# Delta-rule projection: the first half chunk ahead of the small products, a weight split inside the convolution, and a store that is awaited one block later

## What is computed

```python
h = rms_norm(x, mix_norm_w[l])
proj = jnp.einsum('bsd,de->bse', h, w_in[l])
sb_qkv, gdn_qkv, gdn_z, gdn_b, gdn_a, gate_sb, gate_gdn = jnp.split(proj, offsets, axis=-1)
...
qkv = jax.nn.silu(causal_depthwise_conv(gdn_qkv, gdn_conv_w[l]))
...
gq = l2_normalize(gq)
gk = l2_normalize(gk)
beta = jax.nn.sigmoid(gdn_b.astype(f32)).transpose(0, 2, 1)
g = -(jnp.exp(gdn_a_log[l].astype(f32))
      * jax.nn.softplus(gdn_a.astype(f32) + gdn_dt_bias[l].astype(f32))).transpose(0, 2, 1)
o_gdn = gated_delta_rule_chunked(gq, gk, gv, g, beta).transpose(0, 2, 1, 3)
z = gdn_z.reshape(B, S, GDN_HEADS, GDN_HEAD_DIM).astype(f32)
o_gdn = (rms_norm(o_gdn, gdn_out_norm_w[l]) * jax.nn.silu(z)).reshape(B, S, GDN_WIDTH).astype(x.dtype)
```

## Time and profile before

| | us |
|---|---|
| runs: median (lowest to highest), 3 runs | 3376.21 (3370.66 to 3384.74) |
| the profiled execution | 3366.91 |
| its span, first to last instruction | 3365.1 |
| block of `delta_inputs` in the trace | about 1127.5 to 1344.6 |
| block of `delta_rule` in the trace | about 1344.6 to 1568 |

### The profile page before, as it was taken

How to read it: one execution, slowest core, us unless ns; L and a number is a source line. 1 busy time by engine, 2 the same in 40 slices (tenths; PEclk the granted TensorE clock), 3 DMA queues, 4 the chain that set the end, 5 groups by cost and what they waited for, 6 DMA issues and landing times. The chain is left out here.

```text
span 3365.1 us, 30753 instructions
## 1 busy us (share of the span) xinstructions
PE 2814.4 (84%) x10832; PEld 1866.2 (55%) x10832; DVE 1822.0 (54%) x3272; ACT 884.6 (26%) x1621; POOL 1216.2 (36%) x1236
## 2 busy tenths in 40 slices
PE   6999999999899898899999876675767676777777
PEld 5887577765677677898778732232323232322223
DVE  5762643344534564556243786765765566754443
ACT  2113232614446564324223211110111011111111
POOL 0000210000202241540001366666666666666665
PEclk7999999999999999999999988787889788878778
DMA  6452223200221133002223599999999999999998
GB/s 235 174 176 82 71 73 102 88 13 1 88 88 63 40 101 114 6 1 91 95 104 132 210 353 369 373 367 392 363 364 378 373 377 374 364 367 380 369 371 317
DMA packets 228770, 706.46 MB, mean 210 GB/s; under 512 B 23188, under 2 KB 25492, under 8 KB 227735
## 3 DMA queue, kind: packets, MB, share of 16 engines
q0 software_dynamic: 147456, 536.94, 41.6%
q1 hardware_dynamic: 81176, 167.76, 14.5%
HBM read 694.13 MB, written 10.49 MB: 209 GB/s over the span
## 5 line engine op out<-in xcount | busy, mean ns | idle before, releaser
L2825 PE MATMUL work_banks<-rows_over_split,sig 128*128 128x512 f32 x1024 | 520.1, 655 | 238.7 <-issue 170.3
L2825 PEld LDWEIGHTS work_banks<-rows_over_split,sig 128*128 128x128 f32 x1024 | 210.3, 208 | 538.1 <-issue 464.1
L219 DVE TENSOR_TENSOR weights_low<-weights_raw,weights_high 128x2048 fp32r<-128x2048 f32 x108 | 251.3, 2328 | 439.0 <-ACT weights_high L214 429.5
L2825 PE MATMUL work_banks<-weights_raw,sig 128*128 128x512 f32 x512 | 260.1, 666 | 175.7 <-issue 88.2
L2917 DVE CUSTOM_DVE_ANT_0 proj_banks<-rows_over_parts,work_banks 128x1024 f32<-128x1024 f32 x256 | 310.3, 1241 | 161.0 <-DMA rows_over_parts<-in_peer_u_dram,eidx 138.6
L277 PE MATMUL proj_banks<-h_low,weights_high 128*128 128x512 f32 x896 | 358.4, 400 | 30.5 <-DVE weights_low L219 12.9
L214 ACT CAST weights_high<-weights_raw 128x2048 fp32r<-128x2048 f32 x108 | 206.0, 1907 | 612.4 <-PE proj_banks L277 588.1
L277 PE MATMUL proj_banks<-h_high,weights_low 128*128 128x512 f32 x896 | 353.2, 394 | 0.0
L277 PE MATMUL proj_banks<-h_high,weights_high 128*128 128x512 f32 x896 | 352.9, 394 | 0.0
L2711 POOL DMA_INDIRECT rows_over_split<-in_peer_v_dram,eidx x256 | 241.0, 941 | 151.2 <-issue 71.5
L2825 PEld LDWEIGHTS work_banks<-weights_raw,sig 128*128 128x128 f32 x512 | 108.2, 216 | 323.9 <-issue 268.6
(11 more groups left out here) (490 smaller groups left out, 4902.9 us busy)
## 6 DMA issues: line engine op xcount, KB each, us to landing
weights_raw<-in_w_in_dram SPq DMA_DIRECT2D x36, 1024.0 KB, 5.1
weights_raw<-in_ret_w_in_dram SPq DMA_DIRECT2D x24, 1024.0 KB, 5.2
ret_gate<-in_mod_w_dram SPq DMA_DIRECT2D x20, 1024.0 KB
weights_raw<-in_fox_w_in_dram SPq DMA_DIRECT2D x16, 1024.0 KB, 5.3
weights_raw<-in_ret_w_out_dram SPq DMA_DIRECT2D x8, 1024.0 KB, 5.0
weights_raw<-in_peer_w_q_dram SPq DMA_DIRECT2D x8, 1024.0 KB, 5.3
ret_v<-in_mod_w_dram SPq DMA_DIRECT2D x4, 1024.0 KB
weights_raw<-in_fox_w_out_dram SPq DMA_DIRECT2D x4, 1024.0 KB, 5.1
```

The source lines that it names most:

```text
L219: nc.vector.tensor_tensor(wlo[h][:, :, :], raw[h][:, :, :], whi[h][:, :, :].bitcast(F32), ALU.subtract).then_inc(w_split[h], 1)
L2825: last = nc.tensor.matmul(pa[:, half, :], diag[:, s, e, :], v_row(s, e)[:, half * CW:(half + 1) * CW], start=(first and e == 0), stop=(las ...
```

## The change

Three places are rewritten.

1. In `delta_inputs` PE does half 0 of chunk 0 ahead of the small products. ACT and DVE do `split_second` of chunk 0 first of all.
2. On DVE `split_second` of chunk c + 1 stands between tiles 0 and 1 and tiles 2 and 3 of the convolution of chunk c. ACT's order in the loop stays.
3. SP no longer waits for `z_put` in `delta_inputs`. The semaphore is handed to `delta_rule`, where SP waits for it behind the load of the masks, and DVE ahead of its first write of `att`.

```diff
@@ delta_inputs, SP
                     sp.dma_start(z_away, zg[:, :, :]).then_inc(z_put, 16)
-                    sp.wait_ge(z_put, 16)
                     sp.wait_ge(o_put, 16)
@@ delta_inputs, PE (head_squares is only moved up)
+                    project_half(pe, 0, 0, parts)
                     pe.wait_ge(cw_loaded, 16)
...
                     for c in range(n):
-                        project_half(pe, c, 0, parts, c < QKV)
+                        if c:
+                            project_half(pe, c, 0, parts, c < QKV)
@@ delta_inputs, DVE
                     link = Steps(dve, vstep)
+                    split_second(low, 0)
                     dve.wait_ge(wba_high, 1)
...
-                    def convolve(c):
-                        for t in range(4):
+                    def convolve(c, tiles):
+                        for t in tiles:
...
                     for c in range(n):
-                        split_second(low, c)
                         split_next(low, c)
...
                         if c < QKV:
-                            convolve(c)
+                            convolve(c, range(0, 2))
+                        if c + 1 < n:
+                            split_second(low, c + 1)
+                        if c < QKV:
+                            convolve(c, range(2, 4))
@@ delta_inputs, ACT
                     link = Steps(act, astep)
+                    split_second(high, 0)
                     act.wait_ge(wba_loaded, 16)
...
                     for c in range(n):
-                        split_second(high, c)
+                        if c:
+                            split_second(high, c)
@@ delta_inputs and delta_rule
             stage_end(n)
+        return z_put
...
                     sp.dma_start(masks[:, :, :], a["inv_masks"]).then_inc(masks_loaded, 16)
+                    sp.wait_ge(z_put, 16)
...
                         dve.wait_ge(products_full, h + 1)
+                        if h == 0:
+                            dve.wait_ge(z_put, 16)
                         nc.vector.tensor_tensor(att[:, h, :, :], chunks(pb[:, 2, :]), dec[:, h % 2, :, :], ALU.mult)
```

More of the change, by code:

```diff
@@ L1975, in _, with head_squares @@
                 def _(pe):
+                    def head_squares(group):
+                        for i in range(4 * group, 4 * group + 4):
+                            pe.wait_ge(sq_ready, i + 1)
+                            if i >= 4:
+                                pe.wait_ge(ln_done, i - 3)
+                            nc.tensor.matmul(pa[:, i % 4, :], ones, sq[:, i % 4, :], start=True, stop=True
+                                             ).then_inc(ss_full, 1)
+                    project_half(pe, 0, 0, parts)
                     pe.wait_ge(cw_loaded, 16)
@@ L1988, in _ @@
                     last.then_inc(ba_full, 1)
-                    def head_squares(group):
-                        for i in range(4 * group, 4 * group + 4):
-                            pe.wait_ge(sq_ready, i + 1)
-                            if i >= 4:
-                                pe.wait_ge(ln_done, i - 3)
-                            nc.tensor.matmul(pa[:, i % 4, :], ones, sq[:, i % 4, :], start=True, stop=True
-                                             ).then_inc(ss_full, 1)
                     for c in range(n):
-                        project_half(pe, c, 0, parts, c < QKV)
+                        if c:
+                            project_half(pe, c, 0, parts, c < QKV)
                         if 2 <= c < 6:
@@ L2145, in delta_inputs, with delta_rule @@
             stage_end(n)
-    def delta_rule(qkv, sc, sig, osb):
+        return z_put
+    def delta_rule(qkv, sc, sig, osb, z_put):
         H, LV, HG = GDN_HEADS, 7, 4
@@ L3103, in build @@
                 sc = sbuf(st2, "gdn_cols", [P, GDN_HEADS, 5, TT])
-                delta_inputs(parts, qkv, sc, sig, osb, o_away, z_away, columns(a["w_in_2"][0], 7 * D + 2 * GDN_HEADS))
-                delta_rule(qkv, sc, sig, osb)
+                z_put = delta_inputs(parts, qkv, sc, sig, osb, o_away, z_away, columns(a["w_in_2"][0], 7 * D + 2 * GDN_HEADS))
+                delta_rule(qkv, sc, sig, osb, z_put)
                 ogt = x[:, :, :].rearrange("p t (b n) -> p (t b) n", b=2)
```

## The result

| | before | changed |
|---|---|---|
| five runs each: median (lowest to highest), us | 3376.21 (3370.66 to 3384.74) | 3353.85 (3347.24 to 3357.03) |
| profiled execution, us | 3366.91 | 3347.24 |
| block of delta_inputs, first DMA to first DMA of delta_rule | 217.15 | 197.24 |
| block of delta_rule, to the first DMA of gates | 218.89 | 218.78 |

The changed kernel takes 0.9931 of the time of the kernel before (95% interval 0.9919 to 0.9943; the two medians alone give 0.9934): 22.4 us less by the medians, and 19.2 to 27.3 us less by the interval. 3357.0 was forecast, 19.2 us less. The block of delta_rule before ends at 1563.5 in the trace; the "about 1568" given for it ahead of the prediction is too late.

What follows compares the result with a forecast made beforehand. PE was taken to bound delta_inputs, with gains only where it idles or runs at half clock. 6.2 + 5.5 + 1.6 + 5.9 = 19.2 us, so 3376.2 - 19.2 = 3357.0; range 3346 to 3367.

Steps and rivals of the forecast that it cites:

- The start: Start of delta_inputs: half 0 of chunk 0 runs early, the 24 small passes then at full clock; 6.2 us saved.
- Rival (c): Start of delta_inputs: half 0 starts early but not at full clock, 2.7 us less; 16.5 saved, 3359.7; chance 0.10.
- The split: Convolution in delta_inputs: PE no longer loses time to half 1's split; 5.5 us saved in chunk 1, 1.6 in chunk 6.
- The store: End of delta_inputs: the next block no longer waits for the last store; 5.9 us saved.
- Behind the store: Start of delta_rule: store and masks land in time for the first write of att at 1348.15; 0 lost.
- The cause of the late landing: Start of delta_rule: masks and store share SP's rings, consumed in ring order, so the masks land at 1346.4.
- Rival (a): delta_rule: PE's clock falls later, over heads behind the first, costing at most 3.2 us; 16.0 saved, 3360.2; chance 0.15.
- Rival (b): delta_rule: masks come early and the clock stays up, 2.6 to 3.6 us more; 22.3 saved, 3353.9; chance 0.10.
- Rival (d): Chunks 1 to 5 of delta_inputs: the convolution becomes the bound, PE waits for banks; slower, 3382; chance 0.02.

Runs made afterwards that it cites:

- the store alone: Only SP's wait for the store moved into delta_rule, against the kernel before: ratio 0.9987 (0.9977 to 0.9997).
- the start alone: Only the start of delta_inputs changed, split and store wait left as they were, against the kernel before: ratio 0.9976 (0.9966 to 0.9986).

## Why the prediction was right, point by point

**The start.** 6.2 us were summed, 6.6 measured with this part alone. The passes ran at full clock as forecast (0.69 us for three). The wait of 0.77 us for DVE's copy stayed. Rival (c) did not come: an idle time of 1.20 us left the clock at 1.00, as the 1.54 us elsewhere had.

**The split.** 5.5 and 1.6 us were summed, 5.7 and 1.85 measured. The terms came from the distance between two rows, which holds both the idle time and the matmuls at half clock behind it; 3.85 and 1.51, the idle times alone, would have been 2.2 us short of the measured sum.

**The store.** 5.9 us were summed and 5.93 measured (6.70 less 0.77). The next block's first instruction stands 0.77 us behind the issue, as forecast (0.8).

**Behind the store.** The masks were to land 8.45 us behind the store's issue; by their issue at 0.77 and 7.5 us to landing it was 8.3. This term was right in size, and its landing just covered. What it was covered by was not: I let PE start delta_rule at half clock as before, with a first write of `att` 9.4 us behind the start. PE started at full clock and would have released the write at 6.6, as it did where the masks were awaited late, so the masks became the late one. The write came at 8.9, 0.5 us better than forecast, with POOL as the releaser. The forecast had named this row's releaser as a sign that it was wrong, but with a later time, not an earlier one. That delta_rule took what it took before, 218.8 against 218.9 us, is luck and not the reckoned cover: 0.5 us won at the first write, 1.2 lost by the clock over head 1, and 0.9 won behind the heads for a reason that stays open.

**The cause of the late landing.** The Trainium skill, "DMA: Bandwidth & Descriptors", Queues, rings and completion order, has the descriptors of a ring consumed in ring order, from which I made 1346.4 for the masks' landing. The size came out right, 7.5 us instead of 3.2. The cause did not: on ACT's rings it was 7.4. This does not contradict the page, which speaks of the order within one ring; taking the shared ring for the cause of a late load was my step, not the page's. What is left is that both transfers use the same DMA engines, which fits the times but is not shown by itself.

**Rival (a).** It is what the first trace of the changed kernel shows: PE's clock stays up through the first head, PE stands 2.18 us, and the clock falls over head 1. Its price was bounded by 3.2 us; it is 1.24 (6.36 less 5.12), set against 0.5 won at the first write. The same program has shown it and not shown it, and what decides is not known: of the six traces in which the masks are awaited early behind a store in flight (the changed kernel twice, the store alone, the masks on ACT's queue, and the splits ahead of all tiles and behind tile 0), two show it and four have the fall in the first head, where it costs nothing. Where the masks were loaded behind the store's landing, the step to the second write was 6.75 us. The sign named for it, matmuls of 0.43 us spacing in the heads behind head 0, was there; against two in six, a chance of 0.15 was low.

**Rival (b),** masks early and clock up, needed the wait to be moved. With it moved the first write came at 6.55, and delta_rule took 2.3 to 3.5 us less than in the two traces of the changed kernel; 3.1 were worked out. Both traces had the clock up, which is the rival's other condition.

**Rival (d).** It did not come. The rule given against it was that stalls must fill DVE's free time first, 7.6 us of 26, and that it decides only from stalls of 11.5 us a chunk on. As a sum this holds: with the split two tiles earlier DVE stood 10.7 to 11.0 us a chunk for the cast in chunks 2 to 5, its work and stalls came to 29.7 of the 30.2 us, and the block lost 9.9 us. What was wrong is the comfort drawn from it. Stalls of that size looked far off, yet they are two tiles away: 0.4 to 0.9 us with the split behind tile 0, 11 ahead of it. The free time of DVE says what a stall costs, not how soon one comes. That is told by the wait in the ring with the least room, here ACT's for PE: 5.6 us in the changed kernel, 2.5 one tile earlier, where a tile of convolution takes 3.1.

**The total.** 19.2 us were summed, the two blocks show 20.0. The median moved by 22.4 us in this set of runs, by 18.0 where the changed kernel was run again (3364.57 to 3346.60). Where the difference to the blocks goes isn't settled beyond this: delta_inputs began at anything between 1121.0 and 1132.3 us in the twelve traces, though the code ahead of it is the same in all.

## What to carry to other kernels

Cost an idle time by the distance between two rows that enclose it and what follows, not by the bracket: the matmuls at half clock behind it belong to it. When a wait is moved past the end of a block, look at every transfer that the next block issues while the old one is in flight, and ask of each wait on them whether the instruction behind it reads that data; here one wait stood eight heads too early. And when work is moved into a ring of engines that wait for each other, look for the shortest wait in the ring and try the neighbouring places too, since the free time of an engine does not tell how far the cliff is.

## What the runs showed of the hardware that was not expected

Whole sets of runs differ in how fast rows are gathered from memory. The kernel before took 4% less time in two of the four sets than in the other two. The pages of the changed kernel (first) and of the start alone show where: in the last 40% of the span, in which `peer` gathers its rows, the slices move about 370 GB/s in the one and 413 in the other. Whether the chip decides this is not shown: a set at each level ran on a chip of the same number, 9, and the other set at the faster level on number 15.

```profile
GB/s 236 171 181 82 64 76 108 77 25 1 88 89 63 52 89 119 1 1 115 88 120 101 273 351 371 360 376 380 361 364 376 368 374 357 372 373 370 370 369 337
```

```profile
GB/s 231 145 221 92 17 134 74 93 51 1 66 72 110 2 93 79 97 1 1 126 84 112 117 245 404 413 413 414 413 413 414 414 413 413 414 414 414 414 414 302
```

The blocks of this study do not feel it: delta_inputs took 197.25 us in a set at the faster level (split behind tile 0) and 197.24 at the slower one. A kernel's time without the kernel before in the same set says little here.
